# Second block's attentions: first tile's probabilities transposed ahead of the second scores, copies split over two engines, narrower waits

## What is computed

```python
def hybrid_mixer(xn, ...):
    proj = xn @ w_in
    fox = causal_block_attention(fq, fk, fv, log_f_cum)     # key width 64
    fox = rms_norm_2(fox, ...)
    q = (rms_norm_2(c_q, q_norm) @ w_uq); kv = (rms_norm_2(c_kv, kv_norm) @ w_ukv)
    mla = causal_block_attention(q, k, v)                   # key width 96
    mla = rms_norm_2(mla, ...)
    return jnp.concatenate([fox, mla], axis=-1) @ w_o

def causal_block_attention(q, k, v, log_forget_cum=None):   # block i of 128 queries
    s = jnp.einsum('bhqd,bkhd->bhqk', q_i, kf) * scale      # + decay, causal mask
    p = jax.nn.softmax(s, axis=-1)
    return jnp.einsum('bhqk,bkhd->bqhd', p, vf)
```

## Time and profile before

| | |
|---|---|
| time before, median of 3 runs | 2814.84 us (2810.55 to 2817.07) |
| the profiled execution | 2813.48 us |
| its span | 2811.8 us |
| TensorE busy | 2214.5 us, 79% of the span |
| VectorE busy | 1378.6 us, 49% |
| ScalarE busy | 788.5 us, 28% |
| GpSimd busy | 1122.9 us, 40% |
| mean granted clock of TensorE | 0.89 of full speed |
| HBM | 321 GB/s over the span |

### The profile page before, as it was taken

How to read it: one execution, slowest core, us unless ns; L and a number is a source line. 1 busy time by engine, 2 the same in 40 slices (tenths; PEclk the granted TensorE clock), 3 DMA queues, 4 the chain that set the end, 5 groups by cost and what they waited for, 6 DMA issues and landing times. The chain is left out here.

```text
span 2811.8 us, 29004 instructions
## 1 busy us (share of the span) xinstructions
PE 2214.5 (79%) x8948; PEld 1223.7 (44%) x8948; DVE 1378.6 (49%) x2956; ACT 788.5 (28%) x2246; POOL 1122.9 (40%) x1249
## 2 busy tenths in 40 slices
PE   5778886676977978788777676779889987879995
PEld 2455552222333434445324232346555645646663
DVE  5656657775566484555755654433232222432222
ACT  1324323232333334343332343324110111411111
POOL 4015556667666555465566666620011110001111
PEclk9789988889988989899888889889789998879998
DMA  9548889999999999899899999952189985128996
GB/s 354 217 157 336 318 301 405 366 365 404 411 413 407 405 383 386 303 367 352 324 368 370 367 375 372 374 211 75 61 324 420 420 337 185 57 122 326 419 420 267
DMA packets 244866, 902.77 MB, mean 321 GB/s; under 512 B 25522, under 2 KB 32194, under 8 KB 222210
## 3 DMA queue, kind: packets, MB, share of 16 engines
q0 software_dynamic: 157360, 567.05, 52.8%
q1 hardware_dynamic: 87380, 334.23, 30.0%
HBM read 881.27 MB, written 19.92 MB: 321 GB/s over the span
## 5 line engine op out<-in xcount | busy, mean ns | idle before, releaser
L1490 PE MATMUL PS<-arena 128*128 128x512 f32 x2048 | 1038.5, 658 | 350.9 <-issue 169.4
L2086 DVE CUSTOM_DVE_ANT_0 JK<-arena,PS 128x1024 bf16<-128x1024 f32 x512 | 625.0, 1221 | 411.3 <-DMA arena<-in_peer_u_dram,IDX 275.8
L1490 PEld LDWEIGHTS PS<-arena 128*128 128x128 f32 x2048 | 409.8, 209 | 939.6 <-issue 876.1
L878 POOL DMA_INDIRECT arena<-in_peer_v_dram,IDX x512 | 503.9, 984 | 470.7 <-PE PS L1490 261.1
L875 POOL DMA_INDIRECT arena<-in_peer_u_dram,IDX x512 | 493.7, 964 | 335.8 <-DVE IDX L2059 162.5
L911 POOL DMA_DIRECT2D expert_rows<-mod x128 | 67.6, 529 | 640.8 <-DVE mod L2517 393.4
L1048 ACT ACTIVATE ACTV<-DOT 128x1 f32<-128x1 f32 x512 | 101.9, 199 | 756.6 <-DVE DOT L2086 474.9
L1806 PE MATMUL PS<-arena,HT 128*64 128x256 f32 x2048 | 235.1, 382 | 24.1 <-DMA arena<-in_w_down_dram 21.8
L1061 ACT ACTIVATE arena<-IDENT,GACT 128x128 f32<-128x128 f32 x512 | 205.5, 401 | 107.1 <-remote 47.7
L2543 DVE COPY mod<-PS 128x256 f32<-128x256 f32 x64 | 27.2, 425 | 330.4 <-PE PS L1806 330.4
L1806 PEld LDWEIGHTS PS<-arena,HT 128*64 128x64 f32 x2048 | 141.4, 137 | 99.4 <-DMA arena<-in_w_down_dram 26.3
(11 more groups left out here) (342 smaller groups left out, 1881.3 us busy)
## 6 DMA issues: line engine op xcount, KB each, us to landing
arena<-in_w_gate_dram SPq DMA_DIRECT2D x64, 1024.0 KB, 19.2
arena<-in_w_up_dram SPq DMA_DIRECT2D x64, 1024.0 KB, 21.8
arena<-in_w_down_dram SPq DMA_DIRECT2D x64, 1024.0 KB, 17.7
arena<-in_w_ada_dram SPq DMA_DIRECT2D x24, 2048.0 KB, 11.8
arena<-in_w_in_dram SPq DMA_DIRECT2D x11, 2048.0 KB, 16.4
arena<-in_peer_wq_dram SPq DMA_DIRECT2D x10, 2048.0 KB, 8.0
expert_rows<-mod POOLq DMA_DIRECT2D x128, 128.0 KB, 5.5
arena<-in_w_out_dram SPq DMA_DIRECT2D x6, 2048.0 KB, 8.6
```

What stands on the lines that cost most here:

```text
L878: pool.indirect_dma_start(out=GV[b], out_offset=None, in_=v_rows, in_offset=off).then_inc(v_loaded[b], 16)
L1490: last = pe.matmul(PO[:, half, :], DIAG[:, n % DIAGS, :], GV[BUF[n]][:, half * 512:(half + 1) * 512], start=(j == 0), stop=False, skip_gro ...
L2086: dve.tensor_tensor_reduce(JUNK, GU[BUF[n]], HP[tt].rearrange("p b n -> p (b n)"), 1.0, 0.0, ALU.mult, ALU.add, DOT[:, s:s + 1]).then_inc( ...
```

## The change

`values_of` is split in two: `turn_attention`, the transposes of one tile's probabilities, and `values_of`, the value products of one tile. The new order on TensorE is: fox scores, `qmT` and `kmT`, turn of fox tile 0, mla scores, values of fox tile 0, turn and values of fox tile 1, turn and values of mla tile 0, the same of mla tile 1. In tile 1 the four banks are turned in the order 0, 2, 1, 3, heads 0 to 3 for both halves of the keys first; the value products of heads 0 to 3 wait for banks 0 and 2 alone, those of heads 4 to 7 for 1 and 3. In both attentions VectorE copies banks 0 and 1, ScalarE banks 2 and 3. VectorE copies the turned banks of fox tile 0 before it moves the mla scores, and ScalarE makes the exponentials of fox tile 0 before it copies `qmT` and `kmT`. The list of PSUM jobs follows. Both layers do this; the counts of instructions stay the same.

```diff
@@ -220,12 +220,14 @@
 
-    def attend(kind, l, what):
+    def attend_scores(kind, l):
         for tt in range(TT):
             for b in range(2 * (tt + 1)):
-                add((kind + what, l, tt, b), "s" if kind + what == "mpT" else "v")
-            if what == "pT":
-                add((kind + "pv", l, tt), "v")
+                add((kind + "sc", l, tt, b), "v")
+
+    def attend_probs(kind, l, tt):
+        for b in PROB_ORDER[tt]:
+            add((kind + "pT", l, tt, b), "v" if b < 2 else "s")
 
@@ -242,14 +244,19 @@
                 add(("ukv", l, tt, c), "s")
-        attend("f", l, "sc")
+        attend_scores("f", l)
         for name in ("qmT", "kmT"):
...
                     add((name, l, tt, b), "s")
-        attend("m", l, "sc")
-        attend("f", l, "pT")
-        attend("m", l, "pT")
+        attend_probs("f", l, 0)
+        attend_scores("m", l)
+        add(("fpv", l, 0), "v")
+        attend_probs("f", l, 1)
+        add(("fpv", l, 1), "v")
+        for tt in range(TT):
+            attend_probs("m", l, tt)
+            add(("mpv", l, tt), "v")
         halves("byT", l, 0)
@@ -303,6 +310,7 @@
 GATE_BASE = (0, NQ + 1)
+PROB_ORDER = ((0, 1), (0, 2, 1, 3))
 
@@ -961,6 +969,10 @@
                                    accum_out=sums[:, tt, h:h + 1]).then_inc(probs_ready, 1)
+
+            def second_probs(kind, l):
+                for b in (2, 3):
+                    copy_out((kind + "pT", l, 1, b), PT_B[:, 1, 4 * b - 8:4 * b - 4, :], parts(bank((kind + "pT", l, 1, b)), 4))
 
@@ -1262,20 +1274,18 @@
                 prepare(ACT.Exp)
+                exps(0, S_B, NM, DEN)
                 for name, dst in (("qmT", QMT), ("kmT", KMT)):
...
                                      bank((name, l, tt, b))[0:DK].rearrange("p (g t) -> p g t", g=4))
-                for tt in range(TT):
-                    exps(tt, S_B, NM, DEN)
-                for tt in range(TT):
-                    exps(tt, S_M, STATS_M[:, 1], STATS_M[:, 2])
+                exps(1, S_B, NM, DEN)
+                exps(0, S_M, STATS_M[:, 1], STATS_M[:, 2])
+                second_probs("f", l)
+                exps(1, S_M, STATS_M[:, 1], STATS_M[:, 2])
                 ahead_of_root()
-                for tt in range(TT):
-                    for b in range(2 * (tt + 1)):
-                        kt, h = divmod(4 * b, NH)
-                        copy_out(("mpT", l, tt, b), PT_B[:, kt, h:h + 4, :], parts(bank(("mpT", l, tt, b)), 4))
+                second_probs("m", l)
                 for tt in range(TT):
@@ -1637,25 +1647,28 @@
 
-            def values_of(kind, l, S, value):
-                for tt in range(TT):
-                    probs[0] += NH
-                    pe.wait_ge(probs_ready, probs[0])
-                    for b in range(2 * (tt + 1)):
-                        name = (kind + "pT", l, tt, b)
-                        begin(name)
-                        kt, h = divmod(4 * b, NH)
-                        for j in range(4):
-                            last = pe.transpose(bank(name)[:, j * P:(j + 1) * P],
-                                                S[tt][:, h + j, kt * P:(kt + 1) * P], IDENT)
-                        last.then_inc(psum_ready, 1)
-                    begin((kind + "pv", l, tt))
-                    taken(pe, (kind + "pT", l, tt, 2 * (tt + 1) - 1))
-                    for h in range(NH):
+            def turn_attention(kind, l, tt, S):
+                probs[0] += NH
+                pe.wait_ge(probs_ready, probs[0])
+                for b in PROB_ORDER[tt]:
+                    name = (kind + "pT", l, tt, b)
+                    begin(name)
+                    kt, h = divmod(4 * b, NH)
+                    for j in range(4):
+                        last = pe.transpose(bank(name)[:, j * P:(j + 1) * P],
+                                            S[tt][:, h + j, kt * P:(kt + 1) * P], IDENT)
+                    last.then_inc(psum_ready, 1)
+
+            def values_of(kind, l, tt, value):
+                begin((kind + "pv", l, tt))
+                for h in range(NH):
+                    if h % 4 == 0:
                         for kt in range(tt + 1):
-                            last = pe.matmul(bank((kind + "pv", l, tt))[:, h * HD:(h + 1) * HD], PT_B[:, kt, h, :],
-                                             value(kt, h), start=(kt == 0), stop=(kt == tt))
-                    last.then_inc(psum_ready, 1)
+                            taken(pe, (kind + "pT", l, tt, 2 * kt + h // 4))
+                    for kt in range(tt + 1):
+                        last = pe.matmul(bank((kind + "pv", l, tt))[:, h * HD:(h + 1) * HD], PT_B[:, kt, h, :],
+                                         value(kt, h), start=(kt == 0), stop=(kt == tt))
+                last.then_inc(psum_ready, 1)
 
@@ -1729,14 +1742,25 @@
                             last.then_inc(psum_ready, 1)
-                taken(pe, ("kmT", l, 1, 1))
 
...
 
+                def fox_value(kt, h):
+                    return FV[:, kt, h * HD:(h + 1) * HD]
+
+                def mla_value(kt, h):
+                    return KV[:, kt, h, HD:2 * HD]
+
+                turn_attention("f", l, 0, S_B)
+                taken(pe, ("kmT", l, 1, 1))
                 heads_of("m", l, mla_score)
-                values_of("f", l, S_B, lambda kt, h: FV[:, kt, h * HD:(h + 1) * HD])
-                values_of("m", l, S_M, lambda kt, h: KV[:, kt, h, HD:2 * HD])
+                values_of("f", l, 0, fox_value)
+                turn_attention("f", l, 1, S_B)
+                values_of("f", l, 1, fox_value)
+                for tt in range(TT):
+                    turn_attention("m", l, tt, S_M)
+                    values_of("m", l, tt, mla_value)
                 turn_rows("byT", l, 0)
@@ -2361,21 +2385,28 @@
 
+                def probs_copied(kind, l, tt):
+                    for b in PROB_ORDER[tt]:
+                        if b < 2:
+                            name = (kind + "pT", l, tt, b)
+                            arrived(dve, name)
+                            dve.tensor_copy(PT_B[:, 0, 4 * b:4 * b + 4, :], parts(bank(name), 4)).then_inc(evac["v"], 1)
+
                 for tt in range(TT):
                     scored_by("f", l, tt, S_B, MX, NM, HD ** -0.5, causal)
+                probs_copied("f", l, 0)
                 for tt in range(TT):
...
                     scored_by("m", l, tt, S_M, STATS_M[:, 0], STATS_M[:, 1], DK ** -0.5, causal)
-                for tt in range(TT):
-                    for b in range(2 * (tt + 1)):
-                        name = ("fpT", l, tt, b)
-                        arrived(dve, name)
-                        kt, h = divmod(4 * b, NH)
-                        dve.tensor_copy(PT_B[:, kt, h:h + 4, :], parts(bank(name), 4)).then_inc(evac["v"], 1)
-                    valued_by("f", l, tt, 0, DEN, RD)
+                valued_by("f", l, 0, 0, DEN, RD)
+                probs_copied("f", l, 1)
+                valued_by("f", l, 1, 0, DEN, RD)
+                probs_copied("m", l, 0)
                 for tt in range(TT):
                     valued_by("m", l, tt, 512, STATS_M[:, 2], STATS_M[:, 3])
+                    if tt == 0:
+                        probs_copied("m", l, 1)
                     taken(dve, ("mpv", l, tt))
```

## The result

| | before | change |
|---|---|---|
| time, median of 4 runs each | 2813.25 us | 2787.13 us (2773.72 to 2789.45) |
| ratio of the runs | | 0.9896, 95% interval 0.9863 to 0.9930 |
| the profiled execution | 2813.48 us | 2789.45 us |
| its span | 2811.8 us | 2787.8 us |
| TensorE busy | 2214.5 us | 2184.3 us |

The change is 1.0% faster. The forecast said 19 us; the medians differ by 26 us, and the ratio gives 29 us, which puts the time at 2784.0 us, at the lower end of the stated 2784 to 2808 us. The direction was right and the size too small. The two spans differ by 24.0 us, and that difference can be followed row by row. The other 2 to 5 us lie in executions that were not profiled; where, stays open. Two repeats further down gave 24.4 and 19.3 us in the medians.

What follows compares the result with a forecast made beforehand. TensorE's five waits, 8.0 us a layer, mostly on VectorE, bound the attentions. 7.5 and 1.5 us saved a layer make 18 us in both; one more for the clock: 2814.8 - 19 = 2796 us, range 2784 to 2808 us.

Steps and rivals of the forecast that it cites:

- Fox tile 0 turned early, at no cost: Before mla's scores: 8 transposes, 1.04 us, fit the 1.09 us wait; exponentials have 2.4 us of cover; VectorE's copies fit idle time.
- What is late next: Before the values of fox tile 1: VectorE's copy is late; they start at 1958.9 instead of 1966.45 us, 7.5 us saved.
- The later waits: Before mla's value products: 0.1 us left of 0.78, nothing of 0.83; 1.5 us saved; at full clock 0.5 us stays.
- Counted in full to the end: After the attentions: expert loads start when the last output product ends, so the saving counts fully in both layers.
- Between the ends I take today's mixture, and one more us: TensorE's clock in both attention stretches: today's mix gives 18 us; less idle time adds 1 us, 19 us in all.
- The sum of the rows at full clock: Values of fox tile 1 to last value product, without two waits: 12.0 us at full clock, against 16.6 and 20.8 us.
- upper bound of 30.6 us: Both attention stretches: saving if full clock holds throughout, adding 13.4 us less 0.8 us of waits to 18 us.
- The lower bound, 7 us: Both attention stretches: saving left if the clock is low throughout and falls already before the values of fox tile 0.
- Full clock in the whole stretch: Rival, both attention stretches: no idle piece over 1.7 us is left, so the clock stays full; 2784 us, chance 0.17.
- Transposes bring the clock down before mla's scores: Rival: 8 more transposes ahead make mla's 5.51 us of scores take up to 11.0 us; 2808 us, chance 0.03.
- The output products' case: Rival, output products: the clock doesn't come back, up to 20.9 us more a layer; 2850 us, slower, chance 0.03.
- the late turn: Rival: fox tile 0's turn meets an occupied bank or late exponentials; mla's scores slip up to 3.1 us a layer; 2803 us, chance 0.05.

Runs made afterwards that it cites:

- Two repeats further down: The changed kernel, unaltered, run twice more beside the kernel before: medians 2674.2 and 2807.6 us, ratios 0.9913 and 0.9937.
- The kernel before, filled: The kernel before, order untouched, with 32, 10, 4 and 4 identity transposes in its four waits before value products: 2810.1 us, ratio 0.9947.
- the filled change: The change plus 14 identity transposes into an unused PSUM bank before the values of fox tile 1: 2802.3 us, ratio 0.9920 to the kernel before.

## Why the prediction was right and wrong

- *Fox tile 0 turned early, at no cost.* Right, to 0.1 us: scores 4.72 us after the first transpose, ScalarE's cover 2.37 us, no wait at VectorE.
- *What is late next*, the main term of 7.5 us a layer. Right: 7.7 and 7.6 us, and VectorE's copy ends the wait, which is 1.95 us, not 1.7.
- *The later waits*, 1.5 us a layer, with 0.5 us more left at full clock. Right: none in the slow layer, 0.66 us in the fast one.
- *Counted in full to the end.* Right: the first expert load keeps its distance to the last output product, and everything outside the stretches differs by 0.7 us in the net.
- **The step that failed is the clock's, "Between the ends I take today's mixture, and one more us".** The mechanism was in the text; its term was mis-sized. The forecast gave it 1 us. In the first trace the two stretches came out 24.7 us shorter against a sum of 18 us without it: 0.3 us of the difference lies at the start, 6.4 us behind it, where the same steps ran at another clock. The clock was treated as a draw that the order would hardly touch, and the reason given, idle time of 1.9 instead of 8.0 us a layer, was priced at that one us without a row behind it. The kernel before, filled, shows what it is worth: 17.7 us of the old kernel's two stretches were the low clock's, and none of it is left once its waits are filled. The change leaves 5.8 us of it in its first profile. Which of the old waits (4.38 us or the shorter ones) brought the second fall in each layer was not tried one by one.
- *The bounds.* The sum of the rows at full clock, 12.0 us, was right: 12.74 us with the wait of 0.66 us in it. So was the upper bound of 30.6 us: the stretches of the kernel before and of the filled change, at full clock in both layers, differ by 30.5 us. The lower bound, 7 us, no run reached: the clock fell in three layers of six, never before the values of fox tile 1, and was back before the last value product ended. With hindsight, 12.7 us of order and 17.7 us less one slow layer in two give the measured size; that one layer in two falls could not be read from the trace before.
- *Full clock in the whole stretch, 2784 us.* The time by the ratio is this rival's number, but each of the three profiles of the change has one layer at the low clock. As far as the profiles show, the agreement is luck.
- *Transposes bring the clock down before mla's scores.* It didn't happen: in the change 40 transposes stand ahead of the scores, which take 5.51 us in all six layers. Beyond that, transposes of the identity held the clock up. The Trainium skill, "TensorE: Matmul & The Clock Gate", Part 4, says that transposes don't count as busy in the same way; for these f32 transposes the traces differ, with a granted clock of 1.00 in the 44 of them and behind them.
- *The output products' case* and *the late turn* did not occur.

## What to carry to other kernels

Where a matrix engine waits between short steps, price a wait twice: its own length, and what the steps behind it cost at the lower clock, read from rows of the same step at both levels. In the two stretches of the kernel before, the four waits ahead of the value products were 13.7 us long and the low clock cost 17.7 us; of the gain of 24.7 us, 12.0 us are the clock's. Hand a copy to the engine that is idle at that moment, not by a fixed share: all four banks of one tile on ScalarE took the last wait away, where two of four left it. And an idle piece that can't be removed can be filled with transposes that nobody reads, where they end before the wait does.

## What was not expected of the hardware

- An idle piece of 1.95 us behind 5 us of scores and 4 us of short steps was followed by the low clock in three layers of six, with the same instructions and starts equal to 0.01 us; with 2.6 to 3.8 us in all of eight layers in four kernels; with none or 0.42 us there in none of eight. (Waits of 0.66 us stood further on in all eight, and the kernel before, filled, kept full clock with pieces of up to 0.88 us.)
- The same 32 records of value products took 3.76 us at 1.00 and up to 7.06 us where the clock was low. In the change a layer whose clock fell at their start ended its last value product 5.6 to 7.3 us later than one at full clock, through work that had short waits or none.
- The clock need not fall in the wait or right behind it. In the kernel before it was back at 1.00 when the values of fox tile 1 began, behind 0.88 us of idle time, and fell some 2.2 us into these products, with TensorE busy all the time (second layer; PEclk is the third figure from the end):

```profile
2446.00:2447.00 1.00, 1.00 (x11) 1.00 (x11) 0.00 (x0) 0.00 (x0) 0.00 (x0) 0.92 0.00 0
2447.00:2448.00 1.00, 1.00 (x7) 1.00 (x6) 0.00 (x0) 0.00 (x0) 0.00 (x0) 0.50 0.00 0
```

- 14 and 44 transposes of the identity kept the granted clock at 1.00 through waits of 1.95 and 6.36 us.
